# Turning the row tensors with 64x64x64 products, and the first value tile's products inside the last turn of a recurrence

## The chip, the cores and the metric

The kernel runs on one core of one Trainium2 chip. The time is device microseconds of that core for one launch; the lower the better. The kernel before was run three times: 1747.44, 1745.68 and 1744.81 us, median 1745.68. One further execution was profiled; all rows come from it.

## What is computed

One layer of an encoder, 1024 tokens of width 1024. Only the first branch of its time mixer matters here, the recurrence over eight heads of 64 channels:

```python
z = h @ w_in                                   # one projection for both branches
r, k, v, zw, za, zg = shifted parts of z        # token t mixed with token t-1
def step(state, inp):                           # per head, state 64 x 64
    sa = einsum('bhvk,bhk->bhv', state, a_t)
    state = state * w_t + sa (x) b_t + v_t (x) k_t
    return state, einsum('bhvk,bhk->bhv', state, r_t)
y = group_norm(scan(step)) + bonus              # -> gate -> w_branch_a
o = stick_breaking(q_sb, k_sb, v_sb)            # second branch
```

The value tensor `v_sb` of the second branch is a plain product of the modulated input with 512 columns of `w_in`.

## The kernel before, in words

`build` runs six phases one after the other, each a block of its own: start, recurrence, stick-breaking, merge, out, MLP. The change touches `phase_recurrence` (L959 to L1958) alone.

The scan is done in chunks of 64 tokens. One turn (`TURNS` = 8) handles two heads (128 partitions, one head in the lower and one in the upper 64) and 512 tokens, so eight chunks. Its tensors lie channel-major: channels on partitions, tokens along the row. Four of them are also wanted row-major, with tokens on partitions: the values (`vn`), the scaled keys `kh` (`kn`), the scaled writes `bh` (`bn`, which lands in `W[f]`) and the reads `ar` (`an`, which lands in `rhs`). Making them is `natural`: TensorE turns four squares of 128x128 with `pe.transpose` (L1776) into one PSUM bank, and ScalarE copies the bank to SBUF (L1190). The four calls alternate between banks `BA` and `BB`:

```python
def natural(t, name, src, ps):
    for j in range(NT):
        last = pe.transpose(ps[:, j * P:(j + 1) * P], src[:, j * P:(j + 1) * P], ident)
    last.then_inc(s[name + "T"], 1)
```

Each engine's instructions stand in an order written out by hand and unrolled over the eight turns, with counting semaphores between the engines. On TensorE `turn(t)` issues: first products of the turn `M0` (L1812); for the turn before, `queries_maps` (L1738), `state_terms` (L1749, L1754) and `answer_terms` (L1764, L1770); then the inversion of a 64x64 triangle by 32x32 products, `correction` (L1788) and `corrected` (L1797), four rounds of it, each followed by a step of the state's `chain` (L1674) of the turn before and by pieces of `dense` (L1632). `dense` are 24 bf16 products of 128x128x512 that project one half of a later pair's columns; two such units a turn fill the time that the serial inversion leaves. The `natural` calls stand behind `corrected` 1, 2, `squares` (L1654) and `corrected` 3. The turn ends with `X21` (L1892), `T12` (L1902), `mv` (L1908), `outputs` (L1686), `PQ` (L1918) and `variance` (L1703). The dense units are used up when the last turn (7) begins, so it has none.

Behind turn 7 come eight value tiles of 24 products each (L1956), 128 tokens by 512 columns, in banks `BA`, `BB`, `BC`, `BD` in rotation, with the end of the recurrence (`steps`) scattered between them, three places a tile. ScalarE evicts a tile in `value(tt)` (L1309).

The values' weights arrive by DMA, ScalarE cuts their high part in eight pieces (`value_weight`, L1240, four in turn 6, four in turn 7) and GpSimd their low part (`v_lo`, L1111, semaphore `vlo`). In turn 7 the last piece stands on ScalarE directly behind the eviction of `an`; on GpSimd the cuts stand behind `low` (L1092), which waits for the normalised answers. GpSimd ends the phase with `low` and two cuts for the next phase (L154), ScalarE with two splits (L150) and the last value evictions.

Of the kernel before, what the change touches and what calls it, by code (L numbers as in the profile page):

```python
# [10 lines left out]
ACT = mybir.ActivationFunctionType  # L11
ds = bass.ds

P = 128
SEQ = 1024
D = 1024
KT = D // P
TT = SEQ // P
# [3 lines left out]
HD = 64  # L22
# [6 lines left out]
CH = 64  # L29
# [929 lines left out]
def phase_recurrence(nc, g, a):  # L959

    with ExitStack() as es:
        sb = lambda n, s=(P, HALF): es.enter_context(nc.sbuf_tensor(f"rec_{n}", list(s), F32))
        bank = lambda n: es.enter_context(nc.psum_tensor(f"rw_{n}", [P, HALF], F32))
        NB, NT, NC, B = 8, 4, 8, 32
        TURNS = 2 * PAIRS
# [11 lines left out]
                  for at in (PAIRS, PAIRS + 2)] for c in (g.c_hi, g.c_lo))  # L977
# [6 lines left out]
        BAB, BCD, HY = (BA, BB), (BC, BD), (HY0, HY1)  # L984
        per_turn = {"nd": 2, "M1e": 2, "NTd": 2, "NTm": 2, "PQa": NT, "M2e": 2, "TTm": 2, "T12e": 2, "ze": 2, "ge": 2, "ysb": 2, "PQ": 2, "TTe": 4, "Te": 5, "X": 4, "Xe": 4, "TX": 4,
                    "ch": NC, "S": NC}
# [13 lines left out]
        v_stage, v_hi, v_lo = value_weights(g)  # L1000
# [16 lines left out]
        def wait(eng, t, name, j=None):  # L1017
            k = per_turn.get(name, 1)
            if t >= 0:
                eng.wait_ge(s[name], t * k + (k if j is None else j))  # L1020
# [48 lines left out]
        @block.gpsimd  # L1069
        def _(pool):  # L1070

            def front(n):
                wait(pool, n, "cum")
                pool.tensor_tensor(sg[:], cum[:], sg[:], ALU.subtract).then_inc(s["cumE"], 1)
                wait(pool, n, "eN")
                wait(pool, n, "a")
                wait(pool, n - 1, "BT")
                pool.tensor_tensor(aN[:], av[:], eN[:], ALU.mult).then_inc(s["aN"], 1)
                wait(pool, n, "eE")
                wait(pool, n, "kkr")  # L1080
                pool.tensor_tensor(ar[n % 2][:, 0, :], kkr[:], eE[:], ALU.mult).then_inc(s["AT"], 1)
                wait(pool, n, "eI")
                shifted(pool, 0, n)
                pool.tensor_tensor(ar[n % 2][:, 1, :], zs(0, n), eI[:], ALU.mult).then_inc(s["RT"], 1)
                wait(pool, n, "k2")
                wait(pool, n - 1, "M2")
                wait(pool, n - 1, "KhT")
                pool.tensor_tensor(kt_[:], k2[:], eN[:], ALU.mult).then_inc(s["KT"], 1)

            def low(t):  # L1090
                wait(pool, t, "yhi")
                pool.tensor_tensor(out_of(g.c_lo, t), yc[t % 2][:], out_of(g.c_hi, t), ALU.subtract).then_inc(s["ylo"], 1)  # L1092

            def dense_low(d):
                if 2 <= d < DENSE:
                    pool.wait_ge(s["dhi"], d - 1)
                    pool.tensor_tensor(dense_w[d][2], dense_w[d][0], dense_w[d][1], ALU.subtract).then_inc(s["dlo"], 1)

            front(0)
            for t in range(TURNS):  # L1100
                if inside(t + 1):
                    front(t + 1)
                dense_low(t + 2)
                if inside(t - 3):
                    low(t - 3)
                if t >= TURNS - 2:
                    for kt in range((t - TURNS + 2) * PAIRS, (t - TURNS + 3) * PAIRS):
                        pool.wait_ge(s["vhi"], kt + 1)
                        if kt == 0:
                            wait(pool, 3, "bv")  # L1110
                        pool.tensor_tensor(v_lo[:, kt, :], v_stage[kt // 2][:, kt % 2, :], v_hi[:, kt, :], ALU.subtract).then_inc(s["vlo"], 1)  # L1111
            for t in range(TURNS - 3, TURNS):
                low(t)
            for u in range(2):
                cut_next(pool, u)

        @block.scalar
        def _(act):
# [68 lines left out]

            def natural(t, name, dst, ps):
                wait(act, t, name + "T")
                act.activation(dst, ps, ACT.Copy).then_inc(s[name + "e"], 1)  # L1190

# [50 lines left out]
            def turn(t):  # L1242
# [11 lines left out]
                keys(n)  # L1254
                natural(t, "vn", flat(vn[:]), BA[:])
                if t == 0:
# [4 lines left out]
                decays(n)  # L1261
                natural(t, "kn", flat(kn[:]), BB[:])
                dense_high(t + 2)
# [3 lines left out]
                if t == TURNS - 1:  # L1267
                    value_weight(PAIRS + 2)
                natural(t, "bn", W[f][:, :, 1, :].rearrange("p (e j) n -> p j e n", e=2), q4(BA).rearrange("p j (e n) -> p j e n", e=2))
                natural(t, "an", rhs[:, :, 0:HD].rearrange("p (e j) n -> p j e n", e=2), q4(BB).rearrange("p j (e n) -> p j e n", e=2))  # L1270
                if t == TURNS - 1:
# [35 lines left out]
            def value(tt):  # L1307
                act.wait_ge(s["vmm"], tt + 1)
                act.activation(v[tt // 4][:, :, tt % 4 * P:tt % 4 * P + P], (BAB + BCD)[tt % 4][:].rearrange("p (a n) -> p a n", n=P),  # L1309
                               ACT.Copy).then_inc(s["vout"], 1)  # L1310
# [299 lines left out]
        def _(pe):  # L1610
# [6 lines left out]
            def dense(u, first, end):  # L1617
# [16 lines left out]
                if end == 3 * KT:  # L1634
                    mm.then_inc(s["du"], 1)

            def logits(n):
                if not inside(n):
# [134 lines left out]

            def natural(t, name, src, ps):
                for j in range(NT):
                    last = pe.transpose(ps[:, j * P:(j + 1) * P], src[:, j * P:(j + 1) * P], ident)  # L1776
                last.then_inc(s[name + "T"], 1)
# [22 lines left out]
            def turn(t):  # L1800
                f, n, l, ll, lll = t % 2, t + 1, t - 1, t - 2, t - 3
                if t:
                    dense(2 * n, 0, 6)
# [12 lines left out]
                state_terms(l)  # L1816
                answer_terms(l)
                if t:
                    dense(2 * n, 6, 12)
                else:  # L1820
                    dense(1, 0, 16)
# [35 lines left out]
                shifted(pe, 8, t)  # L1857
                natural(t, "vn", zs(8, t), BA)
                if t == 0:
# [9 lines left out]
                wait(pe, t, "KhT")  # L1869
                natural(t, "kn", kh, BB)  # L1870
                chain(l, 4)
# [4 lines left out]
                wait(pe, t, "BhT")  # L1876
                wait(pe, t, "vne")
                natural(t, "bn", bh, BA)
                chain(l, 5)
                dense(2 * n + 1, 13, 18)  # L1880

                corrected(t, 3)
                bonus(ll)
                wait(pe, t, "kne")
                natural(t, "an", ar[f][:, 0, :], BB)
                chain(l, 6)
                dense(2 * n + 1, 18, 24)

                wait(pe, t, "Te")
# [14 lines left out]

                wait(pe, t, "bne")
                for e, j, b in blocks:
# [4 lines left out]

                for name in ("TTm", "T12e", "ane", "mve"):
                    wait(pe, t, name)
# [30 lines left out]
            pe.wait_ge(s["vlo"], KT)  # L1944
            for tt in range(TT):
                if tt == 2:
# [4 lines left out]
                for third in range(3):  # L1951
                    for step in steps.get(3 * tt + third, ()):
                        step()
# [729 lines left out]
```

## Time and profile before

| what | value |
|---|---|
| three runs | 1747.44, 1745.68, 1744.81 us |
| median | 1745.68 us |
| profiled execution, its own time | 1743.47 us |
| its span in the profile | 1741.70 us |
| TensorE busy | 1667.7 us, 96% of the span |
| mean granted TensorE clock | 0.987 |

The span runs from the first to the last instruction; 1.77 us of the execution's own time lie around it. TensorE's matmul records overlap, since a product's record includes its way through the array; what a group really costs its successors is the distance from its start to the next group's start. Weight loads (PEld) are recorded apart from matmuls. A float32 product leaves two matmul records and two weight loads, a float32 transpose one of each. "issue" as the releaser of an idle time means that the engine waited for nothing that the profile shows.

### The profile page before, as it was taken

Reading aid. Unit: us, or ns where it says so; the run is one execution under the profiler, and the core shown is the slowest. Engines: PE = TensorE matmul, PEld = TensorE weight load, DVE = VectorE, ACT = ScalarE, POOL = GpSimd, SP = SyncE. Lnnn points to the kernel's source line nnn. Section 1 sums busy time; section 2 is a strip of 40 time slices with the busy share of each in tenths; the row PEclk is TensorE's granted clock in tenths of the full one; section 3 lists DMA queues with packets and bytes.
Section 4 is the critical chain, followed back from the end, with each engine's and each line's share of the span. In section 5 each row is a group of like instructions: output and inputs, shape, how many; then the busy total and the mean of one; then the engine's idle time right before and its main releaser. Section 6 shows DMA issues by size and latency. Waiting matters only on the chain. (4 is left out here: it accounts for less than half of the span.)

```text
span 1741.7 us, 34694 instructions
## 1 busy us (share of the span) xinstructions
PE 1667.7 (96%) x15178; PEld 859.4 (49%) x15178; DVE 771.3 (44%) x1061; ACT 561.9 (32%) x883; POOL 451.8 (26%) x236
## 2 busy tenths in 40 slices
PE   5999999998999998899999999999999999999997
PEld 2454666666545555444444445444444444444443
DVE  5696666655325455213111487332332323232328
ACT  5323544554325555311312165421212212121300
POOL 2221322222110012023423022651423233232310
PEclk9999999999999999999999999999999999999999
DMA  9851000000010200412110310430202021112002
GB/s 360 284 179 32 15 23 20 4 28 27 27 50 23 62 1 1 145 37 60 48 37 24 109 49 25 141 101 13 84 24 72 24 72 36 60 36 84 1 1 97
DMA packets 105773, 109.69 MB, mean 63 GB/s; under 512 B 2592, under 2 KB 82610, under 8 KB 105394
## 3 DMA queue, kind: packets, MB, share of 16 engines
q1 hardware_dynamic: 105648, 107.82, 19.3%
q8 instruction: 103, 1.69, 0.4%
q14 instruction: 22, 0.18, 0.0%
HBM read 101.52 MB, written 4.19 MB: 61 GB/s over the span
## 5 line engine op out<-in xcount | busy, mean ns | idle before, releaser
L218 PE MATMUL tokens_ps<-a_hi,z 128*128 128x512 bf16 x896 | 231.1, 379 | 0.0
L674 PE MATMUL ff_ps<-ff_hi,c_hi 128*128 128x512 bf16 x512 | 194.0, 379 | 0.9 <-DVE z L2577 0.9
L674 PE MATMUL ff_ps<-ff_lo,c_hi 128*128 128x512 bf16 x512 | 194.0, 379 | 0.0
L674 PE MATMUL ff_ps<-ff_hi,c_lo 128*128 128x512 bf16 x512 | 194.0, 379 | 0.0
L2577 DVE TENSOR_TENSOR z<-ff_ps,z 128x512 f32<-128x512 f32 x128 | 88.3, 690 | 205.0 <-PE ff_ps L674 204.4
L2473 ACT ACTIVATE ff_r<-tokens_ps,cols 128x1024 f32<-128x1024 f32 x30 | 33.4, 1114 | 421.4 <-PE tokens_ps L218 414.4
L2399 POOL TENSOR_TENSOR z<-z 128x1024 bf16<-128x1024 f32 x28 | 62.5, 2232 | 345.9 <-ACT z L2395 345.9
L218 PEld LDWEIGHTS tokens_ps<-a_hi,z 128*128 128x128 bf16 x896 | 87.6, 98 | 105.8
L2565 DVE TENSOR_TENSOR ff_r<-ff_r 128x1024 f32<-128x1024 f32 x32 | 41.1, 1284 | 219.1 <-ACT ff_r L2473 219.1
L218 PE MATMUL tokens_ps<-a_lo,z 128*128 128x512 bf16 x448 | 133.2, 379 | 0.0
L195 POOL TENSOR_TENSOR mg_wlo<-mg_stage,mg_whi 128x1024 bf16<-128x1024 f32 x21 | 45.7, 2178 | 158.1 <-ACT mg_whi L191 158.1
L2510 POOL TENSOR_TENSOR c_lo<-ff_r,c_hi 128x1024 bf16<-128x1024 f32 x32 | 74.9, 2339 | 29.4 <-ACT c_hi L2477 29.4
L218 PE MATMUL mg_ps<-a_hi,mg_whi 128*128 128x512 bf16 x256 | 76.6, 381 | 4.1 <-POOLq L88 4.1
L674 PEld LDWEIGHTS ff_ps<-ff_hi,c_hi 128*128 128x128 bf16 x512 | 50.1, 98 | 61.6 <-issue 1.3
L674 PEld LDWEIGHTS ff_ps<-ff_hi,c_lo 128*128 128x128 bf16 x512 | 50.1, 98 | 60.4
L674 PEld LDWEIGHTS ff_ps<-ff_lo,c_hi 128*128 128x128 bf16 x512 | 50.1, 98 | 60.3
L218 PE MATMUL mg_ps<-a_lo,mg_whi 128*128 128x512 bf16 x256 | 76.9, 382 | 0.0
L218 PE MATMUL mg_ps<-a_hi,mg_wlo 128*128 128x512 bf16 x256 | 76.8, 382 | 0.0
L1632 PE MATMUL rw_front<-a_hi,z 128*128 128x512 bf16 x224 | 74.9, 388 | 0.5 <-DVE const L1355 0.5
L2123 DVE TENSOR_TENSOR mg_ga<-mg_ga,mg_ps 128x1024 f32<-128x1024 f32 x7 | 8.6, 1221 | 143.7 <-PE mg_ps L218 143.7
L805 DVE TENSOR_TENSOR_SCAN b_lo<-z,sb_ahead 128x256 f32<-128x256 f32 (+3 forms) x32 | 53.2, 1704 | 41.7 <-ACT z L909 41.7
L218 PEld LDWEIGHTS tokens_ps<-a_lo,z 128*128 128x128 bf16 x448 | 43.8, 98 | 52.9
(395 smaller groups left out, 3142.8 us busy)
## 6 DMA issues: line engine op xcount, KB each, us to landing
ff_st<-w_ff SPq DMA_DIRECT2D x8, 2048.0 KB, 7.7
z<-w_ff SPq DMA_DIRECT2D x30, 512.0 KB, 4.0
ada_w<-w_ada SPq DMA_DIRECT2D x6, 2048.0 KB, 8.2
z<-w_in SPq DMA_DIRECT2D x18, 512.0 KB, 4.6
z<-w_ada SPq DMA_DIRECT2D x8, 1024.0 KB, 13.5
mg_stage<-w_in SPq DMA_DIRECT2D x16, 512.0 KB, 4.0
zs_stage<-w_in SPq DMA_DIRECT2D x8, 512.0 KB, 7.3
ada_w<-w_ada SPq DMA_DIRECT2D x4, 1024.0 KB, 13.5
```

Of the source, the lines that this page charges most:

```text
L195: pool.tensor_tensor(lo[u][:], stage[u][:], hi[u][:], ALU.subtract).then_inc(lo_ready[u], 1)
L218: last = pe.matmul(out[:, h * HALF:(h + 1) * HALF], w[:, kt, :], a[:, slot, h * HALF:(h + 1) * HALF], start=(x == 0 and y == 0), stop=(x = ...
L674: last = pe.matmul(out, a[:, slot, at], w[:, x, n], start=(x == 0 and y == 0), stop=(x == k - 1 and y == 2))
L805: dve.tensor_tensor_scan(prod[b][:, 0:nk][:, ::-1], m, masked, 1.0, ALU.mult, ALU.max).then_inc(s_scan, 1)
L1632: mm = pe.matmul(unit_bank(u)[:], w_part[:, kt, :], a_part[:, kt, h * HALF:(h + 1) * HALF], start=(x == 0), stop=(x == 3 * KT - 1))
L2123: dve.tensor_tensor(ga[:], ga[:], ps[2][:], ALU.mult).then_inc(s_pa, 1)
L2399: pool.tensor_tensor(ff.lo[u], stage[u], ff.hi[u], ALU.subtract).then_inc(ff.lo_ready[u], 1)
L2473: act.activation(r[u][:], (wide if begun and t >= begun else ps1)[u][:], ACT.Relu, bias=g.cols[:, ds(gr * GT + (b1 + t), 1)]).then_inc(s_r ...
L2510: pool.tensor_tensor(g.c_lo[:, GT * par + t, :], r[u][:], g.c_hi[:, GT * par + t, :], ALU.subtract).then_inc(s_ulo[u], 1)
L2565: dve.tensor_tensor(r[u][:], r[u][:], r[u][:], ALU.mult).then_inc(s_sq[u], 1)
L2577: dve.tensor_tensor(acc, ps2[x % 4], acc, ALU.add).then_inc(s_acc, 1)
```

## The change

1. `natural` makes the same tensor by sixteen products of 64x64x64: the source's 64-column piece of one head is the stationary operand, a 64x64 corner of the identity the moving one. The result is spread over both banks, one head in each. ScalarE empties them with two activations of 128x256.
2. As every call now fills both banks, `kn` waits for `vn`'s evictions, `bn` for `kn`'s, `an` for `bn`'s and `mv` for `an`'s.
3. The first value tile's 24 products are taken out of the loop behind the turns and issued in turn 7 in four pieces of six by `first_value`, into bank `F`. The remaining seven tiles start with tile 1, and `steps` keep their order from there.
4. On GpSimd, in turns 6 and 7, `low(t - 3)` moves behind the low cuts of the value weights.

```diff
-                if inside(t - 3):
+                if inside(t - 3) and t < TURNS - 2:
                     low(t - 3)
                 if t >= TURNS - 2:
                     for kt in ...: pool.tensor_tensor(v_lo[:, kt, :], ...)
+                    low(t - 3)
...
-            def natural(t, name, dst, ps):
+            def natural(t, name, dst):                      # ScalarE
                 wait(act, t, name + "T")
-                act.activation(dst, ps, ACT.Copy).then_inc(s[name + "e"], 1)
+                for e in range(2):
+                    act.activation(dst(e), BAB[e][:, 0:2 * P].rearrange("p (j n) -> p j n", n=HD), ACT.Copy).then_inc(s[name + "e"], 1)
...
+                if tt == 0:                                 # value(tt)
+                    wait(act, end, "HY")
...
+            def first_value(t, first, end):
+                if t < TURNS - 1:
+                    return
+                if first == 0:
+                    pe.wait_ge(s["draw"], UNITS)
+                pe.wait_ge(s["vlo"], end // 3)
+                for n in range(first, end):
+                    kt, (act_part, w_part) = n // 3, ((g.a_hi, v_hi), (g.a_hi, v_lo), (g.a_lo, v_hi))[n % 3]
+                    mm = pe.matmul(F[:], act_part[:, kt, 0:P], w_part[:, kt, :], start=(n == 0), stop=(n == 3 * KT - 1))
+                if end == 3 * KT:
+                    mm.then_inc(s["vmm"], 1)
...
-            def natural(t, name, src, ps):
+            def natural(t, name, src):                      # TensorE
                 for j in range(NT):
-                    last = pe.transpose(ps[:, j * P:(j + 1) * P], src[:, j * P:(j + 1) * P], ident)
+                    for c2 in range(2):
+                        at = (2 * j + c2) * CH
+                        for e in range(2):
+                            last = pe.matmul(BAB[e][rows2[c2], j * HD:(j + 1) * HD], src[heads[e], at:at + CH], ident[heads[e], heads[e]], start=True, stop=True)
                 last.then_inc(s[name + "T"], 1)
...
             def turn(t):
+                first_value(t, 0, 6)                        # ahead of M0
...
                 answer_terms(l)
+                first_value(t, 6, 12)
...
+                wait(pe, t, "vne")
-                natural(t, "kn", kh, BB)
+                natural(t, "kn", kh)
...
-                wait(pe, t, "vne")
-                natural(t, "bn", bh, BA)
+                wait(pe, t, "kne")
+                natural(t, "bn", bh)
                 chain(l, 5)
                 dense(2 * n + 1, 13, 18)
+                first_value(t, 12, 18)
...
-                wait(pe, t, "kne")
-                natural(t, "an", ar[f][:, 0, :], BB)
+                wait(pe, t, "bne")
+                natural(t, "an", ar[f][:, 0, :])
                 chain(l, 6)
                 dense(2 * n + 1, 18, 24)
+                first_value(t, 18, 24)
...
-                wait(pe, t, "bne")
+                wait(pe, t, "ane")                          # ahead of mv
...
-            for tt in range(TT):
+            for tt in range(1, TT):
...
-                    for step in steps.get(3 * tt + third, ()):
+                    for step in steps.get(3 * tt + third - 3, ()):
```

## Rows read from the trace of the kernel before

**Rows 1.** The page's DMA queues: instruction fetches (packets, MB, share).

```profile
q8 instruction: 103, 1.69, 0.4%
```

**Rows 2.** Windows: turns 6, 7, behind them (length, PE, PEld, DVE, ACT, POOL, clock, DMA).

```profile
380.20:419.60 39.40, 37.24 (x1029) 25.52 (x1029) 23.97 (x51) 20.85 (x40) 9.26 (x8) 1.00 0.10 30
419.60:453.60 34.00, 28.27 (x974) 23.18 (x974) 18.38 (x43) 13.16 (x29) 5.09 (x6) 0.90 0.02 4
453.60:507.00 53.40, 52.93 (x463) 27.25 (x464) 16.61 (x31) 10.71 (x21) 7.79 (x8) 1.00 0.15 41
```

**Rows 3.** Timeline of TensorE, turn 6 (start, length): terms in 64x64; transposes with followers.

```profile
381.99 0.64 PE L1749 MATMUL rw_state<-rec_PQ,c_hi 64*64 64x64 f32 x32
382.46 0.65 PE L1754 MATMUL rw_state<-rec_vn,rec_kn 64*64 64x64 f32 x32
...
401.18 0.66 PE L1776 MATMUL rw_main<-const,rec_kh 128*128 128x128 f32 x4
401.76 0.33 PE L1674 MATMUL rw_state<-rec_st,rec_gt 64*64 64x64 f32 x4
```

**Rows 4.** Timeline of TensorE, turns 2 and 7: starts behind an idle time.

```profile
227.40 0.39 PE L1754 MATMUL rw_state<-rec_vn,rec_kn 64*64 64x64 f32 x10 [0.84 <-issue]
...
429.29 0.74 PE L1797 MATMUL rw_invx<-rec_X,rec_TT 32*32 32x32 f32 x35 [1.37 <-issue]
...
441.39 0.65 PE L1788 MATMUL rw_invx<-rec_T,rec_NTm 32*32 32x32 f32 x52 [0.45 <-issue]
```

**Rows 5.** Windows from one such start to the next (columns as in rows 2).

```profile
227.38:231.15 3.77, 3.25 (x127) 2.19 (x127) 3.74 (x10) 0.38 (x1) 0.00 (x0) 1.00 0.02 4
...
437.31:441.37 4.06, 3.61 (x127) 2.36 (x127) 2.72 (x7) 1.65 (x4) 0.00 (x0) 1.00 0.02 4
```

**Rows 6.** Waits of TensorE on "issue", turns 1 to 6 (us, times, longest).

```profile
PE rw_invx L1788 <- issue: 1.6, 3, 0.8
...
PE rw_state L1749 <- issue: 0.3, 1, 0.3
```

**Rows 7.** Window: first three quarters of turn 6 (columns as in rows 2).

```profile
380.18:410.86 30.68, 29.80 (x855) 19.24 (x854) 20.82 (x44) 14.14 (x24) 6.49 (x5) 1.00 0.02 4
```

**Rows 8.** Timeline of TensorE, turn 7 and start of the value tiles.

```profile
419.63 0.62 PE L1812 MATMUL rw_main<-rec_ar,rec_bt 64*64 64x128 f32 x13 [1.31 <-ACT rec_PQ L1296]
...
425.72 0.74 PE L1788 MATMUL rw_invx<-rec_T,rec_X 32*32 32x32 f32 x64 [1.01 <-ACT rec_gt L1199]
...
429.97 1.99 PE L1838 MATMUL rw_main<-rec_ar,rec_kt 64*64 64x128 f32 x32
...
445.69 0.69 PE L1892 MATMUL rw_invx<-rec_T,rec_NTd 32*32 32x32 f32 x32
...
457.04 1.09 PE L1660 MATMUL rw_tail<-const,rec_ri 128*64 128x128 f32 x16 [0.45 <-POOL z L1111]
```

**Rows 9.** Timeline of ScalarE, turn 7: evictions and a weight piece.

```profile
440.47 0.60 ACT L1190 ACTIVATE rec_kn<-rw_main 128x512 f32<-128x512 f32 x1 [2.19 <-PE rw_main L1776]
...
445.53 0.60 ACT L1190 ACTIVATE rec_rhs<-rw_main 128x512 f32<-128x512 f32 x1 [2.06 <-PE rw_main L1776]
446.03 0.62 ACT L1240 ACTIVATE z<-z 128x512 bf16<-128x512 f32 x1
...
451.17 0.66 ACT L1207 ACTIVATE rec_ysb<-rw_state 128x256 f32<-128x256 f32 x2
```

**Rows 10.** Timeline of GpSimd: low cuts of turn 7, the phase's last.

```profile
452.48 4.51 POOL L1111 TENSOR_TENSOR z<-z 128x512 bf16<-128x512 f32 x4
...
510.52 2.13 POOL L154 TENSOR_TENSOR z<-z 128x1024 bf16<-128x1024 f32 x1 [2.18 <-ACT z L150]
```

**Rows 11.** Timeline of TensorE behind the turns: value tile products, gate of the last turn.

```profile
484.11 0.59 PE L1956 MATMUL rw_invx<-z,a_hi 128*128 128x512 bf16 x2
...
484.76 0.59 PE L1956 MATMUL rw_invx<-z,a_hi 128*128 128x512 bf16 x2
...
500.93 1.02 PE L1719 MATMUL rw_tail<-z,rec_g_s 128*128 128x512 f32 x2
```

More of the change, by code:

```diff
@@ L984, in phase_recurrence @@
         BAB, BCD, HY = (BA, BB), (BC, BD), (HY0, HY1)
-        per_turn = {"nd": 2, "M1e": 2, "NTd": 2, "NTm": 2, "PQa": NT, "M2e": 2, "TTm": 2, "T12e": 2, "ze": 2, "ge": 2, "ysb": 2, "PQ": 2, "TTe": 4, "Te": 5, "X": 4, "Xe": 4, "TX": 4,
+        per_turn = {"vne": 2, "kne": 2, "bne": 2, "ane": 2, "nd": 2, "M1e": 2, "NTd": 2, "NTm": 2, "PQa": NT, "M2e": 2, "TTm": 2, "T12e": 2, "ze": 2, "ge": 2, "ysb": 2, "PQ": 2, "TTe": 4, "Te": 5, "X": 4, "Xe": 4, "TX": 4,
                     "ch": NC, "S": NC}
@@ L1254, in turn @@
                 keys(n)
-                natural(t, "vn", flat(vn[:]), BA[:])
+                natural(t, "vn", lambda e: vn[:, :, e * HD:(e + 1) * HD])
                 if t == 0:
@@ L1261, in turn @@
                 decays(n)
-                natural(t, "kn", flat(kn[:]), BB[:])
+                natural(t, "kn", lambda e: kn[:, :, e * HD:(e + 1) * HD])
                 dense_high(t + 2)
@@ L1268, in turn @@
                     value_weight(PAIRS + 2)
-                natural(t, "bn", W[f][:, :, 1, :].rearrange("p (e j) n -> p j e n", e=2), q4(BA).rearrange("p j (e n) -> p j e n", e=2))
-                natural(t, "an", rhs[:, :, 0:HD].rearrange("p (e j) n -> p j e n", e=2), q4(BB).rearrange("p j (e n) -> p j e n", e=2))
+                natural(t, "bn", lambda e: W[f][:, 4 * e:4 * e + 4, 1, :])
+                natural(t, "an", lambda e: rhs[:, 4 * e:4 * e + 4, 0:HD])
                 if t == TURNS - 1:
@@ L1308, in value @@
                 act.wait_ge(s["vmm"], tt + 1)
-                act.activation(v[tt // 4][:, :, tt % 4 * P:tt % 4 * P + P], (BAB + BCD)[tt % 4][:].rearrange("p (a n) -> p a n", n=P),
+                if tt == 0:
+                    wait(act, end, "HY")
+                act.activation(v[tt // 4][:, :, tt % 4 * P:tt % 4 * P + P], ((BAB + BCD)[tt % 4] if tt else F)[:].rearrange("p (a n) -> p a n", n=P),
                                ACT.Copy).then_inc(s["vout"], 1)
@@ L1857, in turn @@
                 shifted(pe, 8, t)
-                natural(t, "vn", zs(8, t), BA)
+                natural(t, "vn", zs(8, t))
                 if t == 0:
@@ L1910, in turn @@
                 outputs(l)
-                for name in ("TTm", "T12e", "ane", "mve"):
+                for name in ("TTm", "T12e", "mve"):
                     wait(pe, t, name)
```

## The prediction

> **What bounds the kernel now.** I read the page first: TensorE is busy 96% of the span. The phases run one after the other, so what counts is how long the recurrence and the value tiles behind it take; a gain or a loss there reaches the end in full. Next, the windows by turn [rows 2]. In turn 6 TensorE is busy 37.24 of 39.40 us, DVE 23.97 and ScalarE 20.85: TensorE sets the length of a full turn. Turn 7, without dense products, takes 34.00 us with TensorE busy 28.27; it is a mixture of TensorE's own work, waits on the serial inversion and a lower clock. Behind it TensorE is busy 52.93 of 53.40 us.
>
> The third view is the one on which this forecast turns. Inside groups without any semaphore in them, TensorE stands still for up to 1.37 us with "issue" as the reason [rows 4]. The windows between two such starts have 127 matmuls and 127 weight loads each [rows 5]: 254 instructions, and the semaphore instructions that the page leaves out make it 256. The DMA list has a queue named "instruction" with 103 packets of together 1.69 MB [rows 1], 16.4 KB a packet, which is 256 instructions at 64 bytes. I read this as: TensorE's program comes in packets of 256 instructions, and where TensorE works through one faster than the next arrives, it waits. Where it waits at both ends, a packet takes 3.77 to 4.06 us [rows 5]. This is 68 instructions per us at most. A group of 64 small products' instructions runs at 64 in 0.47 us (381.99 to 382.46 in [rows 3]), twice that pace; a dense product uses 0.217 us for two instructions (three from 484.11 to 484.76 in [rows 11]), a seventh of it. So dense stretches let the fetch get ahead, small products use the lead up. In turns 1 to 6 this costs 3.8 us in all (the five rows that end on issue, first and last in [rows 6]); in turn 7, which has no dense product, five such waits make 3.2 us (two of them, 1.37 and 0.45, in [rows 4]).
>
> The Trainium skill says otherwise: "Runtime: NRT & Kernel Launch", section Instruction fetch mechanics, has the fetch of the next 16 KiB block hidden behind slow issue. The trace agrees on the block of 256 instructions, not on the hiding. By that rule the sum would be that of the first rival below.
>
> **The change part by part.**
>
> *Turning on TensorE.* Four transposes, start to the next group's start, cost 0.58 us where a chain step follows (401.18 to 401.76 [rows 3]). The new group is not in the trace; its nearest row is `state_terms`, sixteen products of 64x64x64 on the same four quarters of the array: 0.47 us [rows 3]. Bounds: 0.47, and 0.58 if nothing is won. I take 0.48, so 0.10 less per call: four calls in turns 1 to 7, 28 x 0.10 = **-2.8 us**. In turn 0 dense products follow instead of a chain step; I count nothing.
>
> The skill's "TensorEngine Tiling (Array Packing)", Key Properties, says that a change of tiling mode drains the engine; the new group shares the mode of the chain step behind it. This names where the 0.10 comes from and leaves the sum as it is. The same page promises up to twice the speed for each halved dimension; by that alone the group would be several times cheaper, which the 0.47 us does not show, as each float32 product takes two passes and the transpose one.
>
> *Its instructions.* A transpose leaves a matmul and a weight load, a float32 product two of each. A call grows from 8 to 64 instructions: +56, per turn +224. Their execution is in the 0.48 us; their fetch is not. Upper bound: all are paid at the fetch's pace, 224/256 x 3.77 = 3.3 us per turn. Lower bound: 0, if the lead gained in the dense stretches covers them. From M0 to X21, 30.68 us of turn 6, there are 855 + 854 = 1709 instructions [rows 7], which take 25.2 us to fetch: 5.5 us of slack, and the turn still stalls, 3.8 us over six turns, because the small groups lie in lumps. With 224 more the fetch needs 28.5 us of 30.3: the slack falls to 1.8 us. The growth lies in the second half of this stretch, directly behind the groups of the inversion. I take a third of the upper bound, 1.1 us per turn, because the slack shrinks by two thirds but isn't gone: turns 0 to 6, **+7.7 us**.
>
> *Evictions.* Two activations of 128x256 take 0.66 us together, one of 128x512 0.60 [rows 9]: ScalarE, busy half of a turn, hides 0.06. The new waits: `kn`'s eviction starts at 440.47 in turn 7, where the turn is tightest, and would end at 441.13; `bn` comes 1.5 us after that start (441.97). `an` and `mv` have more. Nothing waits: 0. If one margin failed, ScalarE's 0.66 us would be the price of each call.
>
> *The first value tile.* Behind the turns 24 x 0.217 = **-5.2 us**, and the 0.45 us that TensorE now stands there for the last low cut [rows 8] go too: **-0.45**. In turn 7 the four pieces of 1.3 us each come to: the first into the wait of 1.31 us ahead of M0 [rows 8], 0. For this its low pieces must be there: GpSimd has them in turn 6, as `low(3)` no longer stands ahead. The second into the wait of 1.01 us for `gt`, +0.3. The third has no wait beside it, +1.3. The fourth, +1.3, also asks for all eight low pieces. The last high piece stands on ScalarE behind `an`'s eviction: 445.53 + 0.66 + 0.62, then a cut of 4.51/4 = 1.13 us on GpSimd [rows 9, 10], which is about 447.95 where TensorE arrives at 445.69: **2.3 us** of waiting, with X21, T12, mv, PQ queued behind it and the end of the inversion waiting for those. Together **+5.2 us**. The tile as such moves without gain.
>
> *Fetch in turn 7.* 974 + 974 instructions now [rows 2], +224 +48 after: 32.7 us of fetch at 3.77, against 34.0 us of turn. The pieces' 5.2 us bring only 48 instructions and give the fetch time; I take the 3.2 us of stalls as unchanged, 0 (bounds -3.2 and +4.0).
>
> *Clock in turn 7.* The granted clock is 0.90 over the turn [rows 2]: after the idle beginning it falls from the 2.4 GHz level to 1.2 GHz. A mean of 0.90 over 34.00 us is 6.8 us at the lower level; M2's group, 1.99 us long [rows 8], lies in it. If TensorE works in some 4 us of the 6.8, half of them, 2.0 us, is lost. With 2.6 us of dense work ahead of it the fall may not come. Even: **-1.0** (bounds -2.0 and 0).
>
> *The end of the phase.* `steps` keep their order, one tile fewer lies behind them. The gate of turn 7 (500.93 [rows 11]) now has 32 products behind it instead of 56, so TensorE ends 0.86 + 32 x 0.217 = 7.8 us after it. GpSimd's two last cuts hang on the same gate: the second starts at 510.52 after 2.18 us of idle and lasts 2.13 [rows 10]; without the idle it ends 508.34 + 2.13 - 500.93 = 9.5 us after the gate. ScalarE's last value eviction, 0.6 us behind TensorE's end, is out before. The phase now ends on GpSimd: **+0.9 us**.
>
> Sum: -2.8 + 7.7 - 5.2 - 0.45 + 5.2 - 1.0 + 0.9 = **+4.3 us**. The profiled execution took 1743.47 us (span 1741.70 and 1.77 around it), so 1747.8; the median of the runs lies 2.2 us above it, and against it the forecast is 1745.7 + 4.3 = **1750.0 us**, 0.25% slower.
>
> **The rivals.**
>
> *The fetch stays ahead (faster).* No new stall in turns 0 to 6, half of turn 7's stalls covered by the pieces, the clock stays up: -2.8 - 5.65 + 5.2 - 1.6 - 2.0 + 0.9 = -6.0, so 1739.7 us. For it: 25.2 of 30.7 us leave slack, and the six turns have seven such waits in all, not seven a turn. Against it: the added instructions come where TensorE already works through packets at 3.8 to 4.1 us [rows 5]. It decides if the new instructions cost less than about 0.4 us per turn in place of 1.1. This is also the case of the skill's rule above. 0.19.
>
> *Nothing that can be told.* A measurement of this kernel can tell about 0.2%, 3.5 us, from no change. New stalls of 0.5 to 1.0 us a turn give -0.3 to +3.5: 1745 to 1749 us. 0.27.
>
> *The fetch binds (slower than forecast).* Two thirds of the upper bound, 2.2 us a turn, and no help of the clock: 15.4 in place of 7.7 and 0 in place of -1.0: +13, 1758.7 us. For it: four calls within 13 us. 0.12.
>
> *The shared banks make a wait (slower).* Each call of turns 1 to 7 waits 0.3 us for the eviction before it, 28 x 0.3 = 8.4, without new fetch stalls: about +5, 1751 us. Against it: the margins. 0.03.
>
> **How the numbers follow.** The forecast itself, new stalls of about 1.0 to 1.8 us a turn, has 0.39. Slower by over 0.2%: 0.39 + 0.12 + 0.03 = 0.54; within: 0.27; faster: 0.19. The range takes the rivals in but for the far ends of the first and the third: 1741 to 1757 us; the likeliest case alone gives 1749 to 1755.
>
> **What would show it.** In the changed profile: TensorE's issue waits in turns 0 to 6 rise from 3.8 to about 11 us, at distances of 256 instructions; turns 1 to 6 become about 0.7 us longer each. A wait of about 2.3 us on GpSimd's low cut ahead of the last piece in turn 7; no 0.45 us wait behind it. The new group starts 0.48 us ahead of the chain step. The next phase starts after GpSimd's last cut. Wrong it would be if a group of the new products costs well over 0.6 us, or if the stalls only change places.

## The result and the profile after

The changed kernel took 1751.15 us (median of six runs, 1747.11 to 1755.53), the kernel before 1744.51 us beside it (six runs, 1739.03 to 1747.44): a ratio of 1.0043, 95% interval 1.0029 to 1.0057. A second set of runs of both gave 1752.00 against 1742.49 us, 1.0065 (1.0051 to 1.0078). So the change costs 7 to 11 us. The forecast of +4.3 us had the direction and was too small.

The profiled execution was the slowest of its six, 1755.53 us with a span of 1753.5 us. From the page of the changed kernel, the busy times of the engines and the instruction queue:

```profile
PE 1653.4 (94%) x15878; PEld 863.3 (49%) x16074; DVE 770.8 (44%) x1061; ACT 564.1 (32%) x915; POOL 453.6 (26%) x236
...
q8 instruction: 110, 1.80, 0.4%
```

103 packets [rows 1] have become 110. The prediction counted 224 more instructions a turn: 8 x 224 = 1792, and 7 x 256 = 1792. The weight loads rose from 15178 to 16074, by half of it. There are 196 fewer matmuls than weight loads, where the kernel before has as many of each: records are missing. About 50 idle times of 0.16 us among the dense products, put down to issue, are such holes and no time.

The windows of the changed kernel that answer to [rows 2]: turn 6, turn 7, and from there to the end of TensorE's work (length, PE, PEld, DVE, ACT, POOL, clock, DMA):

```profile
388.83:427.85 39.02, 36.69 (x1139) 26.05 (x1147) 24.73 (x51) 20.97 (x44) 11.24 (x9) 1.00 0.08 25
427.85:471.34 43.49, 33.05 (x1102) 24.39 (x1104) 17.90 (x43) 13.51 (x33) 7.13 (x7) 0.88 0.11 33
471.34:526.63 55.29, 54.70 (x464) 28.14 (x470) 16.57 (x31) 11.81 (x23) 6.33 (x5) 1.00 0.07 20
```

Turn 6 is not longer (39.40 before). Turn 7 went from 34.00 to 43.49 us, though only 5.2 us of product were moved into it. (The third window ends elsewhere than that of before; the tiles are compared below.)

For each kernel I took the starts of `M0` of each turn, of the loop's first value product and of the next phase's first product from each trace. The stretches between them, in us, for this kernel and for those of the next section:

| kernel | turns 0 to 6 | turn 7 | value tiles to next phase | sum |
|---|---|---|---|---|
| before | 266.8 | 38.4 | 59.0 | 364.2 |
| changed | 271.4 | 48.2 | 54.6 | 374.2 |
| changed, again | 269.5 | 46.5 | 54.6 | 370.5 |
| prod_only | 269.8 | 39.4 | 58.8 | 367.9 |
| fv_only | 266.3 | 42.7 | 54.6 | 363.7 |
| last_turned | 268.8 | 44.2 | 54.6 | 367.7 |
| last_piece_later | 270.9 | 42.0 | 54.6 | 367.5 |
| two_pieces | 267.4 | 37.1 | 56.2 | 360.7 |
| two_pieces_again | 265.6 | 36.0 | 56.4 | 358.1 |
| turned_later | 265.1 | 38.0 | 54.8 | 357.8 |
| turn_twice | 276.2 | 37.4 | 58.8 | 372.5 |
| prod_twice | 293.2 | 43.1 | 58.8 | 395.1 |

What lies ahead of the first `M0` took 152.2 to 156.4 us in these profiles, in no order that goes with the change (152.9 before, 156.4 in the changed one): 3.6 of the 11.8 us between the two spans are that. Two profiles of one program differ by up to 1.9 us in a stretch (changed and changed again, two_pieces and its repeat), so smaller differences in this table are read with care.

The timeline of TensorE of the changed kernel, turn 7 (start, length, idle time before it in brackets):

```profile
426.62 0.38 PE L1650 MATMUL rw_front<-z,a_hi 128*128 128x512 bf16 x1
...
427.85 1.10 PE L1833 MATMUL rw_main<-rec_ar,rec_bt 64*64 64x128 f32 x32
...
431.88 0.58 PE L1781 MATMUL rw_state<-c_lo,rec_vn 64*64 64x64 f32 x24 [1.00 <-issue]
...
439.22 0.52 PE L1808 MATMUL rw_invx<-rec_T,rec_NTm 32*32 32x32 f32 x37 [1.46 <-issue]
...
442.96 0.62 PE L1796 MATMUL rw_main<-const,z 64*64 64x64 f32 x26 [0.98 <-issue]
...
446.92 0.52 PE L1817 MATMUL rw_invx<-rec_X,rec_TT 32*32 32x32 f32 x37 [0.85 <-issue]
447.37 0.69 PE L1796 MATMUL rw_main<-const,rec_kh 64*64 64x64 f32 x32
447.89 0.30 PE L1691 MATMUL rw_state<-rec_st,rec_gt 64*64 64x64 f32 x4
448.11 0.67 PE L1808 MATMUL rw_invx<-rec_T,rec_NTm 32*32 32x32 f32 x55
450.89 0.36 PE L1808 MATMUL rw_invx<-rec_T,rec_NTm 32*32 32x32 f32 x9 [2.10 <-issue]
...
453.71 1.06 PE L1650 MATMUL rw_front<-z,a_hi 128*128 128x512 bf16 x2
...
461.25 0.63 PE L1650 MATMUL rw_front<-z,a_hi 128*128 128x512 bf16 x1 [2.81 <-POOL z L1111]
...
463.52 0.82 PE L1917 MATMUL rw_invx<-rec_T,rec_NTd 32*32 32x32 f32 x32
```

Three things are to be seen. The issue waits at 439.22, 442.96, 446.92 and 450.89 stand 3.74, 3.96 and 3.97 us apart and cut groups in the middle, where no semaphore is: the arrival of packets, as in [rows 4, 5], now at four boundaries on end. With 431.88 and a small one at 452.86 the waits add to 6.7 us, against 3.2 before. The new group starts 0.52 us ahead of the chain step (447.37 to 447.89). The last piece stands 2.81 us for GpSimd's cut, and is itself stretched: its six products last from 461.25 to 463.52, 2.27 us in place of 1.30, as the third's do (two products in 1.06 at 453.71, where [rows 11] have 0.59).

That wait, on ScalarE and GpSimd of the changed kernel (timelines; evictions of the reads, the high cut, then the low one):

```profile
458.39 0.66 ACT L1192 ACTIVATE rec_rhs<-rw_main 128x256 f32<-128x256 f32 x2 [5.35 <-PE rw_main L1796]
458.93 0.63 ACT L1242 ACTIVATE z<-z 128x512 bf16<-128x512 f32 x1
```

```profile
459.64 1.15 POOL L1111 TENSOR_TENSOR z<-z 128x512 bf16<-128x512 f32 x1 [6.22 <-ACT z L1242]
...
523.98 4.20 POOL L154 TENSOR_TENSOR z<-z 128x1024 bf16<-128x1024 f32 x2
```

And the clock, windows of the changed kernel: turn 7 as a whole up to its `PQ`, and a stretch in its second half:

```profile
427.85:468.15 40.30, 30.11 (x1063) 21.70 (x1065) 17.21 (x42) 10.96 (x26) 5.98 (x6) 0.87 0.12 36
449.00:463.50 14.50, 9.47 (x157) 4.99 (x159) 2.18 (x6) 3.84 (x10) 3.46 (x3) 0.66 0.11 30
```

The drop to the 1.2 GHz level behind `M0`, from 428.0 to 434.8 in the kernel before, is gone. In the six profiles without a piece ahead of `M0` a drop begins between 0.2 us ahead of the turn's `M0` and 8.3 us behind it; in the eight with one, none begins earlier than 13.7 us behind it. In the changed kernel it begins at 450.2, within the stop of 2.10 us (448.8 to 450.9), and lasts 6.8 us; another of 3.4 us begins at 460.5, in the wait for the cut. There it hits dense products.

At the end of the phase the next one's first product waits. Its releaser is ScalarE's sequencer, but GpSimd is the last engine of the phase: its cuts of 4.20 us above end at 528.18, ScalarE's last eviction at 527.26.

```profile
530.63 0.80 PE L850 MATMUL z_ps<-z 64*128 64x128 f32 x4 [4.00 <-ACTq L88]
```

Before, that wait was 3.04 us: +0.96. There ScalarE's last eviction (514.68) came behind GpSimd's cut (512.65).

### The profile page after: what moved, and what is told of

The parts are those of the page before. It is cut to its first block and busy times, and to the rows that moved or that the text cites. A ratio compares the mean times of both kernels' runs of the same rounds, so it can differ in the third digit from the quotient of the medians.

```text
span 1753.5 us, 36324 instructions
## 1 busy us (share of the span) xinstructions
PE 1653.4 (94%) x15878; PEld 863.3 (49%) x16074; DVE 770.8 (44%) x1061; ACT 564.1 (32%) x915; POOL 453.6 (26%) x236
## 5 line engine op out<-in xcount | busy, mean ns | idle before, releaser
L674 PE MATMUL ff_ps<-ff_hi,c_hi 128*128 128x512 bf16 x501 | 189.9, 379 | 1.4 <-DVE z L2602 0.9
L674 PE MATMUL ff_ps<-ff_lo,c_hi 128*128 128x512 bf16 x501 | 189.9, 379 | 0.6
L2540 POOL TENSOR_TENSOR ff_lo<-ff_st,ff_hi 128x1024 bf16<-128x1024 f32 x32 | 68.1, 2159 | 0.0
```

The source lines that it names most:

```text
L674: last = pe.matmul(out, a[:, slot, at], w[:, x, n], start=(x == 0 and y == 0), stop=(x == k - 1 and y == 2))
L2540: pool.tensor_tensor(lo2[par][:, k, :], st2[:, k, :], hi2[par][:, k, :], ALU.subtract).then_inc(s_o2, 1)
```

## The experiments

The theory, from the prediction: what the new products cost is the arrival of their instructions, 64 in place of 8 a call; the moved tile costs mainly the wait for the last low cut. Rivals: the products cost array time or a change of tiling mode; the shared banks and their waits cost; the moved tile, not the products, makes the loss; the issue waits are only unused time that other waits would fill. Ratios are to the kernel before on the same chip; prod_pace and turn_pace were executed once each.

**The two halves alone.** `prod_only` is the change without its first value tile and GpSimd order; `fv_only` is these alone, with the transposes, banks and waits of before.

> The kernel before with the products of 64x64x64 and their evictions and waits, and the first value tile left where it was. Fetch theory (TensorE's program arrives at no more than about 68 instructions per us): turns 0 to 6 grow by some 4.6 us together as in the changed kernel, turn 7 by 2 to 4 us, all of it idle time of TensorE inside groups that wait for nothing, the value tiles by 0; together +7 to +9 us, ratio 1.004 to 1.005. Rival (the four pieces of the first value tile make the loss in turn 7): turn 7 as before, together +4 to +5 us, 1.0025. Rival (the products cost more array time or wait for evictions): the same ratio as the first, but with TensorE's waits on ScalarE or a longer group in place of idle time within groups.

> The kernel before with its transposes, and only the first value tile moved into turn 7 with GpSimd's new order. Fetch theory: 48 instructions more in turn 7 are nothing to the fetch; turn 7 grows by 3 to 5 us (the third and fourth piece 1.3 each, 2.3 to 2.8 for the last low cut, less what a clock that stays up gives), the tiles shrink by 4.5: together -2 to +1 us, ratio 0.999 to 1.0005. Rival (the pieces make turn 7's loss): turn 7 +8 to +10 as in the changed kernel, together +4 to +5, 1.0025.

Measured: prod_only 1747.77 against 1741.70, 1.0035 (1.0022 to 1.0048); fv_only 1742.39, 1.0002 (0.9992 to 1.0013). The products carry the loss; the moved tile gives back in the tiles what it takes in turn 7. The ratio of prod_only lies between what the fetch theory said (1.004 to 1.005) and the rival with turn 7 as before (1.0025), and its interval holds both: the waits have to decide. The waits of TensorE in turn 7 of prod_only (us, times, longest):

```profile
PE rw_main L1780 <- issue: 2.8, 3, 1.4
PE rw_invx L1792 <- issue: 1.6, 1, 1.6
PE rw_main L1816 <- ACT rec_PQ L1297: 1.3, 1, 1.3
...
PE rw_invx L1801 <- issue: 0.6, 1, 0.6
```

and of fv_only:

```profile
PE rw_front L1649 <- POOL z L1111: 2.9, 2, 2.4
PE rw_invx L1804 <- issue: 1.5, 1, 1.5
PE rw_state L1780 <- issue: 0.5, 1, 0.5
```

In prod_only TensorE stands 5.0 us on issue in turn 7 (3.2 before), 2.8 of them at the products' own group (L1780), and no row names the evictions of `vn`, `kn`, `bn` or `an`: the shared banks cost nothing. In fv_only the issue waits fell to 2.0 us in these rows (3.2 before), but the low cut costs 2.9. Turn 7 grew by 1.0 in the one, by 4.3 in the other and by 8.0 to 9.8 with both: the parts do not simply add.

**Each group issued twice.** The second time writes the same values again.

```diff
-                for j in range(NT):
+                for j in list(range(NT)) * 2:
```

in front of the transposes of before (`turn_twice`) and in front of the products of prod_only (`prod_twice`).

> The kernel before with every group of four transposes issued twice: 8 instructions and about 0.47 us of array time more per call, 32 calls. Both theories: +15 to +16 us, ratio 1.009; hardly new idle time within groups (256 instructions more in all).

> The kernel with the products only (first value tile where it was), every group of sixteen products issued twice: about 0.46 us of array time more per call as with the transposes, but 64 instructions in place of 8. Fetch theory: against the kernel with the products once +22 to +28 us, as each turn then asks for 2550 instructions, 37.5 us of fetch in a turn of 39; against the kernel before 1.017 to 1.020. Rival (array time): +15 against the products once, 1.013 against the kernel before.

Measured: turn_twice 1752.79, 1.0067 (1.0054 to 1.0080), +11.1 us between the medians for 256 more instructions (one packet more); prod_twice 1773.91, 1.0189 (1.0172 to 1.0205), 26 us above prod_only for 2048 more instructions (eight packets, page of prod_twice below; the timeline shows one doubled group and what follows it).

```profile
q8 instruction: 118, 1.93, 0.5%
```

```profile
255.41 1.16 PE L1780 MATMUL rw_main<-const,rec_kh 64*64 64x64 f32 x64
256.39 0.30 PE L1675 MATMUL rw_state<-rec_st,rec_gt 64*64 64x64 f32 x4
```

Array time alone would be 32 x 0.46 = 15 us (a doubled group takes 0.98 us, a single one 0.52); 8 packets x 3.77 are 30. The 26 us lie within the forecast of the fetch theory, but they are not fetch alone. The listed issue waits of turns 0 to 7 rose by 3.9 us over prod_only's (15.1 for 11.2, holes left out), and the lower clock level lasted some 30 us in them in place of 7. By the kernel before, where 6.8 us of that level cost some 2.4 us in turn 7 (its groups against the same ones at the higher level), 23 us more of it would be about 8 (an estimate). Why the level came more often, no run shows. The transposes stay under their array time (32 x 0.47 = 15 us): the issue waits of turns 1 to 7 shrank to 2.7 us, from 7.1 before.

**The pace by itself.** One call in turn 7, the one for the reads, with 16 times its products (`prod_pace`) or transposes (`turn_pace`), everything else as in prod_only or before.

```diff
-                for j in range(NT):
+                for j in list(range(NT)) * (16 if (t, name) == (TURNS - 1, "an") else 1):
```

> The kernel with the products only; in turn 7 the group for the reads is issued sixteen times in a row instead of once: 1024 instructions without a wait in them. Fetch theory: TensorE works at the pace at which its program arrives, 3.8 us per 256 instructions, so the group takes about 14 to 15 us. Rival (array time): 16 x 0.46 = 7.4 us.

> The kernel before; in turn 7 the four transposes of the reads are issued sixteen times in a row: 128 instructions. Both theories: 16 x 0.47 = 7.5 us, with at most one idle time of the fetch in it.

The timeline of TensorE in prod_pace:

```profile
450.91 3.37 PE L1780 MATMUL rw_main<-const,rec_ar 64*64 64x64 f32 x156
455.16 2.10 PE L1780 MATMUL rw_main<-const,rec_ar 64*64 64x64 f32 x128 [0.88 <-issue]
458.90 2.10 PE L1780 MATMUL rw_main<-const,rec_ar 64*64 64x64 f32 x128 [1.65 <-issue]
462.65 1.67 PE L1780 MATMUL rw_main<-const,rec_ar 64*64 64x64 f32 x98 [1.65 <-issue]
...
464.17 0.33 PE L1675 MATMUL rw_state<-rec_st,rec_gt 64*64 64x64 f32 x3
```

and in turn_pace:

```profile
444.76 7.15 PE L1776 MATMUL rw_main<-const,rec_ar 128*128 128x128 f32 x64 [0.27 <-issue]
451.84 0.33 PE L1674 MATMUL rw_state<-rec_st,rec_gt 64*64 64x64 f32 x4
```

This settles the mechanism. There is no semaphore in the group, yet TensorE stops every 128 matmuls and 128 weight loads. 455.16 to 458.90 and to 462.65 are 3.74 and 3.75 us a packet: 2.10 us of work and 1.65 us of nothing. Sixteen calls' worth takes 13.3 us as products (450.91 to 464.17), a little less than the 14 to 15 expected; as transposes it takes 7.1 us without a stop. Within a packet the products start 0.47 us a call apart, so by array time sixteen calls would take 7.6 us, 0.5 more than the transposes; the rest is arrival, and up to 452.8, in the first stretch, the lower clock level. The DMA view of the same 13.3 us (450.9 to 464.2) has four packets of the instruction queue, which start 3.6 to 3.8 us apart:

```profile
q8 instruction: 4, 0.07, 2.5%
```

2.5% of sixteen engines' 13.3 us are 1.3 us a packet. So the transfer itself fills a third of the 3.75 us; what fills the rest no run shows.

The Trainium skill ("Runtime: NRT & Kernel Launch", Instruction fetch mechanics) has the fetch hidden behind slow issue; this trace shows no stop among the transposes, which ask for 128 instructions in 7.1 us, and the fetch bare for the products. Its "TensorEngine Tiling (Array Packing)", Theoretical Speedup, gives small tiles up to twice the speed for each small dimension; here 7.6 us of array work stands against 7.1.

The executions took 1762.84 and 1748.16 us against 1746.60.

**The change again, and two variants of turn 7.** `after_again` is the changed kernel. `last_turned` has the products in turns 0 to 6 and transposes in turn 7, into one bank:

```diff
             def natural(t, name, src):                      # TensorE
+                if t == TURNS - 1:
+                    for j in range(NT):
+                        last = pe.transpose(BA[:, j * P:(j + 1) * P], src[:, j * P:(j + 1) * P], ident)
+                    last.then_inc(s[name + "T"], 1)
+                    return
```

`last_piece_later` moves the fourth piece behind the turn's other products:

```diff
                 dense(2 * n + 1, 18, 24)
-                first_value(t, 18, 24)
...
                 variance(ll)
+                first_value(t, 18, 24)
```

> The changed kernel once more, to be compared with the three below on the same chip, and for a second look at turn 7, whose profile showed 9.8 us more than before where the products alone make 1.0 us there and the first value tile alone 4.3. If the two parts add up, turn 7 lasts 43 to 44 us in this profile and the ratio is 1.004; if they feed each other (stalls of the fetch, the lower clock level, pieces slowed by it), it is again 46 to 49 us and the ratio 1.005 or more.

> The changed kernel with the 128x128 transposes back in turn 7 alone (into one bank, emptied by the same two activations), products in turns 0 to 6, first value tile in turn 7. Fetch theory: turn 7 has 224 instructions less, its idle time within groups falls by 2 to 4 us, so 0.9975 to 0.999 of the changed kernel, about 1.002 of the kernel before. Rival (the shared banks' waits or the pieces make the loss): as the changed kernel, 1.004.

> The changed kernel with the last piece of the first value tile issued at the end of turn 7, behind the variance, where all eight low cuts are long there. My step (TensorE stands 2.3 to 2.8 us for the last low cut): turn 7 shortens by 2 to 3 us, 0.998 to 0.999 of the changed kernel. Rival (the wait is cover for the fetch and for the inversion, which are late anyway): no shorter than 1 us less, the time comes back as idle time elsewhere in the turn.

Measured: after_again 1752.00 against 1742.49, 1.0065 (1.0051 to 1.0078); last_turned 1747.08, 1.0043 (1.0027 to 1.0059); last_piece_later 1747.73, 1.0038 (1.0023 to 1.0053). Turn 7 of after_again took 46.5 us, so the two parts feed each other. Against after_again the medians stand at 0.997 (last_turned) and 0.998 (last_piece_later), near what the fetch theory and the step of the cut had said; last_turned is not at 1.002 of the kernel before, though. The waits of TensorE in turn 7 of last_piece_later:

```profile
PE rw_invx L1808 <- issue: 2.8, 2, 1.7
PE rw_state L1781 <- issue: 1.3, 1, 1.3
PE rw_invx L1817 <- ACT rec_X L1187: 0.5, 1, 0.5
```

The low cut's wait has gone and turn 7 is 4.5 us shorter than in after_again: 2.8 for the wait and 1.8 from fewer issue waits (4.1 for 5.9). The clock has no visible share: its lower level lasted 6.8 us in turn 7 of both, here from 438.0. last_turned kept a wait of 3.4 us for the cut (0.6 more), but its issue waits fell to 3.1 us (2.8 less): with fewer instructions it won 2.2 us in turn 7. Neither is back at the kernel before, since both keep the products in turns 0 to 6.

**Only what has its data.** `two_pieces` is the kernel before with two pieces of the first value tile in turn 7, ahead of `M0` and behind `answer_terms`; the other twelve products stay in the loop. No piece waits for a low cut of turn 7.

```diff
+                first_value(t, 0, 6)                        # ahead of M0
...
+                first_value(t, 6, 12)                       # behind answer_terms
...
-                    for n in range(KT * third, KT * third + KT):
+                    for n in (range(KT * third, KT * third + KT) if tt else range(12 + 4 * third, 16 + 4 * third)):
```

> The kernel before with its transposes and only the first two pieces (twelve products) of the first value tile in turn 7, where TensorE waited 1.31 and 1.01 us; the other twelve products behind the turn as before, in bank F, with GpSimd's new order. My account: 2.6 us of work go into waits and 0.45 us of waiting for the last cut goes too, 0.3 us is late: -2.5 to -3, and up to 2 us more if the clock stays at its upper level; 0.9975 to 0.9985 of the kernel before. Rival (turn 7's length is set by the inversion and the fetch, so that pieces put there only lengthen it): 1.000 or more.

Measured: 1740.89 against 1742.49, 0.9991 (0.9980 to 1.0002). Turn 7 is 1.3 us shorter than before and the tiles 2.8. The waits ahead of `M0` (1.31) and for `gt` (1.01) are gone and the one for `X` fell from 1.0 to 0.5 us: the pieces lie in them, as the prediction had them (0 and +0.3). There is no drop of the clock in this turn. But its issue waits are 4.5 us (3.5 in the repeat below), in place of 3.2, though it has 24 instructions more and no new products.

**The version that follows.** `turned_later`: transposes with their two banks as before, three pieces where the change puts them, the fourth behind `variance`. `two_pieces_again` ran beside it.

> The kernel before with its transposes; the whole first value tile in turn 7, its last piece at the turn's end, behind the variance. Turn 7 should last 38.5 to 40 us (42.7 with the last piece where the changed kernel has it), the tiles 54.6: together with turns 0 to 6 as before -3 to -4.5 us, 0.9975 to 0.998. Rival: what the pieces bring behind the turn they cost within it, 1.000.

> The kernel with two pieces once more, for a narrower interval: its profile has 3.5 us less from the first M0 to the stick-breaking phase than the kernel before, its runs gave 0.9991 with an interval that holds 1. If the 3.5 us are real: 0.998 to 0.9985. If they are the lower clock level alone, which comes in some executions and not in others: 0.999 to 1.000.

Measured: turned_later 1736.80 against 1742.25, 0.9972 (0.9964 to 0.9981); two_pieces_again 1738.09, 0.9980 (0.9970 to 0.9991). Both beat the kernel before, turned_later by slightly more than forecast; between them the intervals overlap. Windows of turned_later for turn 6, turn 7 up to the loop's first value product, and from there to the next phase:

```profile
380.71:419.88 39.17, 38.38 (x1035) 25.93 (x1035) 24.96 (x51) 20.76 (x40) 10.96 (x9) 1.00 0.08 25
419.88:457.84 37.96, 34.49 (x1169) 26.30 (x1169) 18.96 (x47) 14.09 (x32) 7.43 (x7) 1.00 0.13 38
457.84:512.64 54.80, 50.80 (x295) 24.30 (x295) 16.11 (x28) 12.14 (x22) 7.89 (x5) 1.00 0.07 20
```

With a whole value tile in it, turn 7 is 0.5 us shorter than before, at a clock of 1.00 in place of 0.90. Part of the gain is thus the absent drop, which cost the profiled execution of the kernel before some 2.4 us. The issue waits in it are 2.5 us:

```profile
PE rw_invx L1804 <- issue: 1.2, 1, 1.2
PE rw_state L1780 <- issue: 0.5, 1, 0.5
...
PE rw_state L1690 <- issue: 0.5, 1, 0.5
PE rw_invx L1813 <- issue: 0.3, 1, 0.3
```

turned_later and last_piece_later differ by the products (with their banks and evictions) alone: 0.9972 and 1.0038, 0.66% or 11 us (9.7 between the profiles: 5.9 in turns 0 to 6, 4.0 in turn 7). In prod_only the same products cost 6 us. Their price depends on what dense work, waits and clock surround them.

## Why the prediction was right in direction and too small

The measured 1751.15 us lies close to the forecast 1750.0, but part of that is luck: turns 0 to 6 were overpriced by 1.4 us, turn 7 was underpriced by 4.6 to 6.4.

*What bounds the kernel: right.* Packets of 256 instructions, about 3.75 us each; prod_pace shows it in one group.

*Turning on TensorE: -2.8 predicted.* The group costs 0.52 us in place of 0.58, not 0.48. 28 x 0.06 is -1.7: 1.1 us too hopeful. The row taken for it, `state_terms`, stands behind another group of the same form, the new group behind a different one. In a stream of its own kind it takes 0.47 (prod_pace).

*Its instructions, turns 0 to 6: +7.7, with the turning +5.3.* The five kernels with products there took 268.8 to 271.4 us, the mean 270.1; the five with single transposes (before, fv_only, two_pieces, its repeat, turned_later) 265.1 to 267.4, the mean 266.2. That is +3.9, of which the turning is -1.4: fetch costs 5.3, where 7.7 was said. Right in kind, two thirds in size. This 5.3 is what is left over, not a sum of waits. The issue waits of the changed kernel there did not rise to 11 us. They rose from 3.8 to 6.8 (turns 1 to 6, holes left out, as above; the three largest of the six rows):

```profile
PE rw_invx L1808 <- issue: 2.3, 4, 0.9
...
PE rw_state L1781 <- issue: 1.6, 3, 0.6
...
PE rw_state L1771 <- issue: 1.0, 1, 1.0
```

Nor is each turn 0.7 us longer: turns 0 to 3 took 0.8, 1.7, 2.4 and 0.4 us more, turns 4 to 6 0.2 to 0.4 less, and in after_again turn 1 took 0.7 less. A likely reason, not shown, is that the borders of the packets shift from turn to turn, and with them whether a stop hits something that waits anyway.

*Evictions, 0: right.* No row of TensorE's waits in turns 1 to 7 of the changed kernel or of prod_only names these evictions.

*First value tile.* The tiles gave -4.4, where -5.2 for the tile and +0.9 for the end made -4.3: right (the 0.45 us of the last cut's wait went from the stretch of turn 7). The end came at +0.96; the prediction's own figures, 9.5 - 7.8 - 0.6, make 1.1. In turn 7 the first piece cost nothing, and the second's +0.3 shrank since it also covered 0.5 us of the wait for `X`. The wait for the low cut was 2.8 in place of 2.3: the piece stood on ScalarE where it was expected, the cut ended at 460.79, and the product started 0.46 us behind that, which the prediction left out.

*Fetch in turn 7, 0: this is the term that failed.* "The pieces' 5.2 us bring only 48 instructions and give the fetch time; I take the 3.2 us of stalls as unchanged." They rose to 6.7 us (5.9 in after_again), +2.7 to +3.5, close to the upper bound of +4.0. Single profiles scatter: with transposes in turn 7 the issue waits are 2.2 to 4.5 us (before, fv_only, both with two pieces, last_turned, turned_later), with products once 4.1 to 6.7 (prod_only, last_piece_later, the changed kernel twice), so about 2.2 us more on average. The count gave a warning: 32.7 us of fetch against 34.0 of turn leave 1.3 us. And the pieces do not give the fetch as much time as their length: the first two took the place of waits of 1.31 and 1.01 us, in which the fetch could run already. two_pieces agrees, with 4.5 and 3.5 us of issue waits in place of 3.2.

*Clock, -1.0: wrong.* The drop behind `M0` went, as hoped, but a new one came in the 2.10 us stop, with another in the wait for the cut. The third and fourth piece took 2.27 us each in place of 1.30, +1.0 apiece, and the groups beside them some 1.5 more (by their distances from start to start, against the same groups at the higher level). Measured the same way the drop of the kernel before cost 2.4 us (2.0 in the prediction), so the clock made about +1.1. In the three kernels without any drop in turn 7 (two_pieces, its repeat, turned_later) the longest stop of TensorE there is 1.2 to 1.3 us; in the five others with a piece ahead of `M0` each drop begins in, or up to 1.7 us behind, a stop of 1.7 to 2.8 us. The sum of the stops does not sort them: two_pieces has as much issue wait as last_piece_later. That the stops bring the drop is likely, not shown; if so, the clock term hung on the fetch term, and they should have been priced together.

Turn 7 of the changed profile, summed: fetch +3.5, cut +2.8, pieces 5.2 less 3.5 of waits that went (1.3 ahead of `M0`, 1.0 for `gt`, 0.5 for `X`, 0.5 for the last cut, 0.2 on DVE), clock +1.1, turning -0.2: +8.9, measured +9.8. Of the 0.9 left, 0.3 are two idle times of 0.16 us and some 0.3 a stop inside L1677's group (475.1 to 475.5) that the list of waits doesn't have. The prediction's terms for this stretch make +3.4 (5.2 - 0.45 - 1.0 - 0.4).

*The rivals.* "The fetch stays ahead" fell by prod_only and prod_pace, and with it the Trainium skill's rule ("Runtime: NRT & Kernel Launch", Instruction fetch mechanics) as it would act here. "The shared banks make a wait" fell: none is there. "The fetch binds" was half right, in turn 7 rather than turns 0 to 6.

prod_only lengthens turn 7 by 1.0 us only, though its issue waits rise by 1.8: its lower clock level there lasts 3.4 us in place of 6.8, and the wait for `gt` is 0.4 shorter. Left open is why both halves together cost 3 to 4.5 us more there than the sum of each. The clock drop's place is a likely reason; no run holds the clock fixed.

## What to carry to other kernels

Price small float32 products by their number of instructions as well as by array time: here a rewrite that saves 0.06 us of array and adds 56 instructions lost in the turns with dense work (3.9 us over seven) and in the one without. Waits filled with work are no new time for the fetch. Move work into a wait only where its operands exist: the same tile was worth nothing in fv_only, where its last piece stood for a cut, and 5 us in turned_later, where that piece came at the end of the turn. Look behind each long stop on TensorE for the granted clock, and for the products that run at it.

## What the runs showed of the hardware

Instructions reach TensorE at 256 per 3.75 us in an unbroken stream (prod_pace), 68 per us, while 256 such instructions execute in 2.10 us; the packet's transfer takes 1.3 us of it. Four float32 transposes of 128x128 cost 0.44 us in a long stream (7.1 us for 64) and 0.58 among others; the sixteen products of 64x64x64 that replace them 0.47 in a stream and 0.52 among others. So a group of transposes pays 0.14 us once, a group of products 0.05. The Trainium skill ("TensorEngine Tiling (Array Packing)", Key Properties) has a change of tiling mode drain the engine; measured from a group's start to the next group's start, such a drain can have cost no more than these 0.14 us here, and no run separates it from the rest.

The granted clock's drop, which began 8.3 us behind the turn's `M0` in the kernel before, begins no earlier than 13.7 us behind it in the eight profiles with 1.3 us of dense products ahead of `M0`, and not at all in three of them. In the changed kernel it begins 22.4 us behind `M0`, 1.4 us into a stop of 2.1 us.
